# First weights in two halves, unit 60's weights split sooner, final norm weight on ScalarE, stacked transposes inside a unit, in a two-layer hybrid decoder trunk

## The reference

```
h = rmsnorm(x) * norm_w
z, xBC, dt, q, k, v, g_ret, u, g_pool = split(h @ w_in)      # 1024 -> 5648
y_ssd  = rmsnorm(ssd(silu(conv(xBC)), softplus(dt)) * silu(z))
y_ret  = rmsnorm(retention(rotary(q), rotary(k), v)) * silu(g_ret)
y_pool = (multiscale_pool(u) @ pool_w) * silu(g_pool)
x = x + concat(y_ssd, y_ret, y_pool) @ w_out                 # 2048 -> 1024
```

## Time and profile before

| | us |
|---|---|
| median of 3 runs | 967.36 (965.58 to 969.66) |
| the profiled execution | 967.27 |
| its span in the trace | 965.5 |
| TensorE matmul busy | 947.5 |
| VectorE busy | 693.6 |
| ScalarE busy | 419.3 |
| mean granted TensorE clock | 0.994 of full speed |

### The profile page before, as it was taken

The page is one execution under the profiler, slowest core; times in us unless marked ns, Lnnn a source line. Parts: engine busy times, 40 slices in busy tenths (PEclk is TensorE's granted clock), DMA queues, the critical chain, the costliest instruction groups (busy, mean ns, idle before and its releaser), DMA issues.

```text
span 965.5 us, 18839 instructions
## 1 busy us (share of the span) xinstructions
PE 947.5 (98%) x7974; PEld 906.6 (94%) x7974; DVE 693.6 (72%) x944; ACT 419.3 (43%) x701; POOL 45.4 (5%) x148
## 2 busy tenths in 40 slices
PE   8999999999999999999999999999999999999996
PEld 7999999999999889999999999999989988899995
DVE  6899677857896568664558967787679757686445
ACT  6432454234775135532334235533267633544222
POOL 0000011010010000000000001011101000000000
PEclk9999999999999999999999999999999999999999
DMA  7234221234234453423333242221533451652222
GB/s 268 104 115 146 81 67 49 69 108 155 88 107 153 153 204 123 142 91 109 132 127 113 87 143 64 67 67 50 157 107 103 136 198 63 224 202 66 88 66 99
DMA packets 38277, 113.33 MB, mean 117 GB/s; under 512 B 11088, under 2 KB 13776, under 8 KB 36784
## 3 DMA queue, kind: packets, MB, share of 16 engines
q1 hardware_dynamic: 37936, 111.23, 34.7%
q0 software_dynamic: 256, 0.88, 0.3%
HBM read 94.63 MB, written 17.47 MB: 116 GB/s over the span
## 4 chain that ended last, share of the span: by engine, by line
PE 90%; DVE 5%; ACT 3%; DMA 1%; issue 1%; SPq 0%; DVEq 0%; ACTq 0%
PE acc L534 26%; PE acc L536 25%; PE acc L535 25%; PE misc L638 2%; PE misc L624 1%; DVE w_lo L1156 1%; ACT w_hi L888 1%; PE misc L691 1%; PE misc L641 1%; DMA x<-in_x 1%; PE misc L713 1%; PE acc L781 1%; PE misc L762 1%; PE misc L732 1%; PE misc L655 1%; PE misc L610 1%
## 5 line engine op out<-in xcount | busy, mean ns | idle before, releaser
L534 PE MATMUL acc<-hin,w_hi 128*128 128x288 f32 x1536 | 461.4, 300 | 0.9 <-DVE w_lo L1156 0.9
L536 PE MATMUL acc<-hin,w_lo 128*128 128x288 f32 x1536 | 453.8, 295 | 0.0
L535 PE MATMUL acc<-hin,w_hi 128*128 128x288 f32 x1536 | 453.7, 295 | 0.0
L534 PEld LDWEIGHTS acc<-hin,w_hi 128*128 128x128 f32 x1536 | 289.5, 188 | 13.6 <-issue 10.8
L888 ACT ACTIVATE w_hi<-w_raw 128x1024 fp32r<-128x1024 f32 x122 | 129.0, 1057 | 381.8 <-PE acc L536 378.6
L535 PEld LDWEIGHTS acc<-hin,w_hi 128*128 128x128 f32 x1536 | 289.5, 188 | 0.4
L536 PEld LDWEIGHTS acc<-hin,w_lo 128*128 128x128 f32 x1536 | 289.5, 188 | 0.0
L1156 DVE TENSOR_TENSOR w_lo<-w_raw,w_hi 128x1024 fp32r<-128x1024 f32 x122 | 148.8, 1220 | 126.5 <-ACT w_hi L888 126.4
L534 PE MATMUL acc<-mix,w_hi 128*128 128x288 f32 x416 | 124.0, 298 | 4.0 <-DVE w_lo L1156 1.7
L536 PE MATMUL acc<-mix,w_lo 128*128 128x288 f32 x416 | 122.6, 295 | 0.0
L535 PE MATMUL acc<-mix,w_hi 128*128 128x288 f32 x416 | 122.5, 294 | 0.0
(11 more groups left out here) (212 smaller groups left out, 1045.2 us busy)
## 6 DMA issues: line engine op xcount, KB each, us to landing
w_raw<-in_w SPq DMA_DIRECT2D x122, 512.0 KB, 3.6
decay<-cum_rows SPq DMA_DIRECT2D x8, 1024.0 KB, 6.0
h<-in_ssm SPq DMA_DIRECT2D x16, 512.0 KB, 6.3
out_ssm_s<-h SPq DMA_DIRECT2D x16, 512.0 KB, 6.2
x<-in_x SPq DMA_DIRECT2D x8, 576.0 KB, 6.9
x_kept<-x SPq DMA_DIRECT2D x4, 576.0 KB, 2.8
x<-x_kept SPq DMA_DIRECT2D x4, 576.0 KB, 5.8
out_y<-x SPq DMA_DIRECT2D x8, 288.0 KB, 2.2
```

The lines of the kernel that those rows point to most:

```text
L534: pe.matmul(out, wh, hi, start=k == 0, stop=False)
L535: pe.matmul(out, wh, lo, start=False, stop=False)
L536: return pe.matmul(out, wl, hi, start=False, stop=k == KT - 1)
```

## The change

- The block of unit 0 is loaded in two halves of four k steps, the first ahead of x; each half is made high and split by itself, and the second half comes behind chunk 1 of x. ScalarE and VectorE take the first two squares ahead of unit 1's weights. `project_first` waits for the halves apart.
- In layer 1's step of unit 58, `high` and `split` of unit 60's weights come first in the step.
- ScalarE multiplies each chunk of the last x by final_norm_w right behind its square, by chunk for units 53 to 58 and by half for the last two. `out_of` multiplies two chunks at once by rstd alone.
- The five stacked transposes run inside unit 13, behind its third product. VectorE's two copies to `tokv` move from its step 12 to its step 13.

```diff
@@ -262,6 +262,9 @@
         s_st = sem("small_states_loaded", 32)
+        w0_in = sem("first_w_part_loaded")
+        w0_hi = sem("first_w_part_high")
+        w0_lo = sem("first_w_part_split")
         w_hid = sem("w_high", UNITS)
@@ -358,6 +361,7 @@
         sum_half = sem("last_norm_sum")
+        x_weighted = sem("final_weights_in")
         rstd_half = sem("last_norm_rstd")
@@ -477,10 +481,14 @@
             sp.dma_start(vec[:, :], a["vec"][0]).then_inc(vec_in, 16)
+            first, rest = slice(0, KT // 2), slice(KT // 2, KT)
+            sp.dma_start(w_raw[:, 0, first, :], a["w"][0][:, first, :]).then_inc(w0_in, 16)
             for i in range(4):
                 sp.dma_start(x[:, 2 * i:2 * i + 2, :], a["x"][:, 2 * i:2 * i + 2, :]).then_inc(s_x[i], 16)
-                if i < 2:
-                    load(i)
+                if i == 0:
+                    sp.dma_start(w_raw[:, 0, rest, :], a["w"][0][:, rest, :]).then_inc(s_raw[0], 16)
+                if i == 1:
+                    load(1)
             for l in range(DEPTH):
@@ -507,7 +515,7 @@
                 for i in range(4):
-                    sp.wait_ge(f_ok, KT * half + 2 * i + 2)
+                    sp.wait_ge(f_ok, 4 * half + i + 1)
                     sp.dma_start(a["y"][:, 2 * i:2 * i + 2, c], x[:, 2 * i:2 * i + 2, c]).then_inc(f_out, 16)
@@ -545,7 +553,9 @@
                             pe.wait_ge(*of(p_lo, k + 1))
-                        if k == 0:
+                        if u == 0 and k == 0:
+                            pe.wait_ge(w0_lo, 1)
+                        elif k == (0 if u else KT // 2):
                             pe.wait_ge(*of(w_split, u + 1))
@@ -782,6 +792,15 @@
+            def stacked_turn():
+
+                pe.wait_ge(*of(tab_in, 16))
+                pe.wait_ge(*of(stk_ok, 1))
+                for t in range(TILES):
+                    src = stk[:, cols(t)] if t < TILES - 1 else gm[0:96, 0, :]
+                    mm = pe.transpose(mb[:, t // 4, (t % 4) * 96:(t % 4 + 1) * 96], src, ident[0:96, 0:96])
+                mm.then_inc(stk_T, 1)
+
             def project_last():
@@ -822,7 +841,9 @@
                         pe.wait_ge(*of(pool_out, u - U_GPOOL - 1))
-                    if u == S_RST:
+                    if u == S_RET:
+                        project(u, stacked_turn, 2)
+                    elif u == S_RST:
                         project(u, ret_inter)
@@ -855,13 +876,6 @@
                         pool_mm_(u - U_GPOOL - 1)
-                    if u == S_STK:
-                        pe.wait_ge(*of(tab_in, 16))
-                        pe.wait_ge(*of(stk_ok, 1))
-                        for t in range(TILES):
-                            mm = pe.transpose(mb[:, t // 4, (t % 4) * 96:(t % 4 + 1) * 96], stk[:, cols(t)] if t < TILES - 1 else gm[0:96, 0, :],
-                                              ident[0:96, 0:96])
-                        mm.then_inc(stk_T, 1)
                     if S_RET <= u < S_RST:
@@ -1009,15 +1023,21 @@
             eng.wait_ge(*of(vec_in, 16))
+            eng.wait_ge(w0_in, 16)
+            go(act(w_hi[:, 0, 0:KT // 2, :], w_raw[:, 0, 0:KT // 2, :], ACT.Copy), w0_hi, 1)
             for j in range(KT):
+                if j == 2:
+                    eng.wait_ge(*of(s_raw[0], 16))
+                    go(act(w_hi[:, 0, KT // 2:KT, :], w_raw[:, 0, KT // 2:KT, :], ACT.Copy), w_hid, 1, 0)
+                if j == 4:
+                    square(0, 0)
+                    square(1, 0)
+                    high(1)
                 if j % 2 == 0:
                     eng.wait_ge(*of(s_x[j // 2], 16))
-                if j in (1, 4):
-                    high(j // 4)
                 raw_high(j, 0)
-            for j in range(KT):
-                if j >= 2:
-                    eng.wait_ge(*of(sq_add, j - 1))
+            for j in range(2, KT):
+                eng.wait_ge(*of(sq_add, j - 1))
                 square(j, 0)
@@ -1025,6 +1045,9 @@
                     m = u - U_OUT - OUT_CHUNKS
+                    ahead = l == DEPTH - 1 and u == UNITS - 3
+                    if ahead:
+                        high(whole(l, u) + 2)
                     if m >= 0:
@@ -1034,9 +1057,12 @@
                         square(m, l + 1)
+                        if l + 1 == DEPTH:
+                            settle()
+                            go(act(x[:, m, :], x[:, m, :], ACT.Copy, scale=T("fnw")[:, m:m + 1]))
                     if u == 0 and l:
                         norm_rstd(l)
-                    if whole(l, u) + 2 < DEPTH * UNITS:
+                    if whole(l, u) + 2 < DEPTH * UNITS and not ahead:
                         high(whole(l, u) + 2)
@@ -1126,6 +1152,9 @@
                    sq_half, 2 * half + m - (KT - 2) + 1)
+                settle()
+                go(act(halves(x[:, m, :])[:, half, :], halves(x[:, m, :])[:, half, :], ACT.Copy,
+                       scale=T("fnw")[:, m:m + 1]), x_weighted, 2 * half + m - (KT - 2) + 1)
@@ -1563,11 +1593,20 @@
             eng.wait_ge(*of(vec_in, 16))
+            eng.wait_ge(w0_hi, 1)
+            go(V.tensor_tensor(w_lo[:, 0, 0:KT // 2, :], w_raw[:, 0, 0:KT // 2, :],
+                               w_hi[:, 0, 0:KT // 2, :].bitcast(F32), ALU.subtract), w0_lo, 1)
             for j in range(KT):
-                if j in (1, 4):
-                    split(j // 4)
+                if j == 2:
+                    eng.wait_ge(*of(w_hid, 1, 0))
+                    go(V.tensor_tensor(w_lo[:, 0, KT // 2:KT, :], w_raw[:, 0, KT // 2:KT, :],
+                                       w_hi[:, 0, KT // 2:KT, :].bitcast(F32), ALU.subtract), w_split, 1, 0)
+                if j == 4:
+                    add_square(0, 0)
+                    add_square(1, 0)
+                    split(1)
                 raw_low(j, 0)
-            for j in range(KT - 1):
+            for j in range(2, KT - 1):
                 add_square(j, 0)
@@ -1576,7 +1615,8 @@
                     o = u - U_OUT
-                    if o < OUT_CHUNKS and whole(l, u) + 2 < DEPTH * UNITS:
+                    ahead = o < OUT_CHUNKS or l == DEPTH - 1 and u == UNITS - 3
+                    if ahead and whole(l, u) + 2 < DEPTH * UNITS:
                         split(whole(l, u) + 2)
@@ -1591,7 +1631,7 @@
                                 add_square(m, l + 1)
-                            if whole(l, u) + 2 < DEPTH * UNITS:
+                            if not ahead and whole(l, u) + 2 < DEPTH * UNITS:
                                 split(whole(l, u) + 2)
@@ -1689,22 +1729,22 @@
                 eng.wait_ge(rstd_half, half + 1)
-                settle()
-                for j in range(first, end):
-                    xh = halves(x[:, j, :])[:, half, :]
-                    go(V.scalar_tensor_tensor(out=xh, in0=xh, scalar=T("fnw")[:, j:j + 1],
-                                              in1=halves(rstd[:, :])[:, half, :], op0=ALU.mult, op1=ALU.mult),
-                       f_ok, KT * half + j + 1)
+                eng.wait_ge(x_weighted, 2 * half + 2)
+                settle()
+                r = halves(rstd[:, :])[:, half, :].unsqueeze(1).to_broadcast([P, 2, HALF])
+                for i in range(first, end):
+                    two = x[:, 2 * i:2 * i + 2, half * HALF:(half + 1) * HALF]
+                    go(V.tensor_tensor(two, two, r, ALU.mult), f_ok, 4 * half + i + 1)
...
             square_of(1)
-            out_of(0, 5, 0)
+            out_of(0, 2, 0)
             x_of(KT - 1, 1)
-            out_of(5, KT, 0)
-            out_of(0, KT, 1)
+            out_of(2, 4, 0)
+            out_of(0, 4, 1)
             lane.close()
...
         @block.gpsimd
```

## The result

The changed kernel takes 975.07 us (median of 6 runs, 973.43 to 977.87), the kernel before 967.28 (6 runs): a ratio of 1.0084, 95% interval 1.0068 to 1.0099. The forecast was 971.1, in a range up to 975.0. It is slower by 7.8 us where 3.8 were forecast; the profiled execution has a span of 972.5 against 965.5.

The account below looks back on a forecast made before the run. TensorE's matmuls were taken as the bound, filling 947.5 of 965.5 us, so only changes to its gaps count. The sum 5.4 + 0 - 1.6 = +3.8 us on 967.27 gave 971.1 us, range 968.8 to 975.0.

Parts of the forecast that it names:

- Part 1's stall: Stacked transposes moved into unit 13: TensorE stalls 3.41 us before the retention turn, less 0.69 gained; +5.4 us for two layers.
- the case in which the clock holds: The main forecast, 971.1 us, own range 969.5 to 972.6: no clock fall in unit 13's new stall; chance 0.55.
- the fall as a rival: Clock falls in the stall behind unit 13, slowing turn and unit 14: 972.6 to 974.1, up to 976; chance 0.33.
- The 3.0: Kernel's end: about 3.0 us from TensorE's last work to the slow-clock stretch; taken as the gap that decides a fall.
- The price: Loss per clock fall behind unit 13's stall: 1.5 us, at half the speed, judged from warm-up matmul records.
- The 3 us of slow clock: Behind unit 13's stall, the assumed duration of slow clock after a fall, costing 1.5 us.
- The forecast for two falls: Clock falls in the stalls of both layers: 974.1 us, the forecast if the Trainium skill's warning is followed.
- Part 2: First weights in halves, at the start: 0 us, bounds -0.9 to +0.5, since unit 0's k = 4 starts as now.
- the text's own 1.2 us: At the start, how far the first product comes forward (9.93 before, near 8.7 forecast); the sum takes nothing for it.
- Parts 3 and 4: At the end, unit 60's weights sooner and final norm weight on ScalarE: together -1.6 us, bounds -0.8 to -2.1.
- part 3: Near the end, unit 60's high and split come sooner; it starts at 944.23 instead of 945.00: -0.77 us.

Follow-up runs that it names:

- stall_part: The changed kernel with 6 matmuls on ones behind unit 13; no total time given, turn to output 10.05 us in both layers (one execution).

## Why the prediction was wrong

- **Part 1's stall held to 0.03 us.** Forecast 3.41 less 0.69, 2.72 per layer; measured 2.74 or 2.75 in four layers of two versions. Copies behind split(15), split behind high(15), high behind unit 13: each step stands in the profile, and moving the copies removes it.
- **The step that failed is the one that kept the clock out of the sum.** The forecast took the case in which the clock holds as the likeliest (0.55) and the fall as a rival (0.33), with "the gap of 3.2 is barely longer" than 3.0 as the reason against. The 3.0 was the delay after a last burst at the end of the kernel, and was read as a threshold; even by it the forecast gap of 3.2 would have lost the clock. And it isn't one: the clock fell 2.2 us after the last product in the changed kernel's layer 0, and behind only 2.05 us of idle time in stall_part. It fell in all 6 profiled stalls of the three versions that have one. The rule of the Trainium skill (TensorE: Matmul & The Clock Gate, on HAM oscillation), that after such a gap the next burst starts cold, was the better forecast. The trace agrees that the gap loses the clock, but not that the burst starts cold: in five of the six stalls the turn began at 2.4 GHz and lost it 0.9 to 1.4 us later.
- **The price was right for five of six falls.** 1.5 us per fall were forecast, from six records a microsecond against 11; that row gives the clock as 1.00, but between 111 and 112 the changed profile has six records beside a clock of 0.50. The 3 us of slow clock had no row behind them. Five falls, with the clock slow for 3.4 us, cost 1.56 to 1.61; the one in the changed kernel's layer 0, where it was slow from 105.6 to 112.5, cost 2.59. The forecast for two falls, 974.1, is 1.0 under the measured median.
- **Part 2 was right in the sum and wrong in what it left out.** The halves give 0, as worked out, though several times on the way were not (the first half was high at 3.90, chunk 0 of x landed at 5.95 and not at 6.95). But the text said itself that four k steps come forward and k = 4 does not, so the gap ahead of k = 4 had to grow, by the text's own 1.2 us, from 1.4 to 2.6 us, and no step asked what that does to the clock. The gap was 1.8 to 2.2 us in the profiles, and the clock fell behind it in 4 of 6: their norm sum starts at 23.9 us on average, against 22.3 in the two that held. With 1.82 us, the profiled execution of the changed kernel was one where it held.
- **Parts 3 and 4**: -1.6 forecast, -1.69 to -1.73 measured in every version that has both. The split into -0.77 and -0.8 was coarser than that: alone they give -0.40 and -0.54, since the weight's activation delays the high that part 3 puts first.

The mean granted clock closes the account. (1 - clock) x span over the 6 runs of the changed kernel, with a mean clock of 0.9895, is 10.2 us, and over 23 runs of the kernel before, with 0.9939, 5.9 us. This counts slow time in which TensorE is idle too, so it is an upper estimate of the loss. Of the 8.4 us between the two means 4.3 are clock by it, and 4.1 are work and waits, against the 3.8 that the sum had.

## What to carry over

Moving an operation earlier on one engine is worth nothing if its consumer stays behind a wait in another engine's program: look at what the step there begins with, and whether that waits for the very unit that should hide it. Count a stall of the matrix engine of 2 us or more twice, once for itself and once for the slow clock behind it (it came in all 6 stalls of 2.05 and 3.4 us here, at 1.6 to 2.6 us each); and when the first operands come earlier but the next ones don't, a gap grows, and the clock can fall behind it too. To tell a part of 1 us in runs that spread by 4, cut profiled executions at matmuls that all versions have.

## What the hardware showed

The clock falls in the kernel before as well, while TensorE is called busy. Behind the sample retention (L732, 128 matmuls of 64 x 8 in 3.9 us) it is slow for some 3.4 us:

```profile
188.00:190.00 2.00, 2.00 (x59) 1.98 (x56) 1.84 (x3) 0.00 (x0) 0.13 (x2) 0.95 0.07 16
190.00:192.00 2.00, 2.00 (x10) 2.00 (x10) 1.94 (x4) 0.00 (x0) 0.18 (x1) 0.50 0.00 0
192.00:194.00 2.00, 2.00 (x13) 2.00 (x12) 1.11 (x1) 0.00 (x0) 0.00 (x0) 0.70 0.00 0
```

From the first matmul of L732 to the first of L750 it takes 11.9 us in 16 of the 26 layers profiled, 13.4 in 7 and 10.4 in 3, and the clock is slow there for 3.4, 6.8 and 0 us: steps of 1.5 us, and they differ between executions that do the same work there. This, twice per execution, is probably much of why the times of the unchanged kernel spread from 964.8 to 969.7, with mean clocks of 0.996 to 0.990. It wasn't tried to keep the clock up there.
